# Loading a transformer block's small inputs from the ACT queue at the start, ahead of the first weight tiles

## The reference

```python
# every sub-layer: x <- LayerNorm(ALPHA * x + gate(c) * f(x * (1 + scale(c)) + shift(c)))
def even_mixer(h, positions, w_in, conv_w, a_log, dt_bias, gdn_norm_w, sinks, w_out):
    a_qkv, a_z, a_a, a_b, b_q, b_k, b_v = split_cols(h @ w_in, EVEN_WIDTHS)
    a_qkv = jax.nn.silu(causal_conv(a_qkv, conv_w))
    ...
    g = -jnp.exp(a_log) * jax.nn.softplus(a_a + dt_bias)
    beta = jax.nn.sigmoid(a_b)
    o_a = gated_delta_rule(a_q, a_k, a_v, g, beta)
    ...
    q = rotary(b_q, positions, SWA_ROT_DIM, ROPE_THETA)
    ...
    o_b = sink_window_attention(q, k, v, sinks)
    return jnp.concatenate([o_a, o_b], -1) @ w_out
```

## Time and profile before

| | |
|---|---|
| median of 3 runs | 1677.35 us (1676.88 to 1677.6) |
| profiled execution, its own time | 1677.35 us |
| its span | 1675.4 us |
| TensorE busy | 1604.0 us, 96% |
| VectorE busy | 1289.5 us, 77% |
| ScalarE busy | 1009.6 us, 60% |
| GpSimd busy | 104.6 us, 6% |
| bytes moved | 515.33 MB, mean 308 GB/s |

### The profile page before, as it was taken

The page is one execution under the profiler, slowest core; times in us unless marked ns, Lnnn a source line. Parts: engine busy times, 40 slices in busy tenths (PEclk is TensorE's granted clock), DMA queues, the critical chain, the costliest instruction groups (busy, mean ns, idle before and its releaser), DMA issues.

```text
span 1675.4 us, 20080 instructions
## 1 busy us (share of the span) xinstructions
PE 1604.0 (96%) x7810; PEld 1288.9 (77%) x7810; DVE 1289.5 (77%) x1176; ACT 1009.6 (60%) x868; POOL 104.6 (6%) x78
## 2 busy tenths in 40 slices
PE   4999999999999999699999999999999999999996
PEld 1876766888778887488888888888888888888875
DVE  1766466755566666889899898898988898988987
ACT  1442335444445554477777777777777777777765
POOL 0003120200001102100000000000000000000004
PEclk9999999999999999799999999999999999999998
DMA  9688696855535445399999999999999999999993
GB/s 347 230 298 310 246 326 214 286 178 201 201 134 179 157 164 181 133 377 399 369 389 381 377 389 369 387 387 369 387 387 369 387 383 374 388 382 364 386 382 134
DMA packets 234370, 515.33 MB, mean 308 GB/s; under 512 B 8936, under 2 KB 40960, under 8 KB 234176
## 3 DMA queue, kind: packets, MB, share of 16 engines
q1 hardware_dynamic: 228688, 493.77, 80.5%
q0 software_dynamic: 3008, 10.20, 1.8%
q10 hardware_dynamic: 2576, 10.02, 1.7%
HBM read 507.15 MB, written 13.11 MB: 311 GB/s over the span
## 4 chain that ended last, share of the span: by engine, by line
PE 90%; DVE 4%; DMA 3%; ACT 1%; issue 1%; POOL 0%; ACTq 0%; POOLq 0%; SPq 0%; DVEq 0%
PE bank L756 27%; PE bank L758 27%; PE bank L757 27%; DMA ring<-in_cond_w 2%; PE bank L735 2%; PE bank L927 2%; PE bank L1193 1%; DMA small<-in_ev_w_in 1%; PE bank L1105 1%; PE bank L1175 0%; PE bank L751 0%; DVE w_lo L1681 0%; ACT hT_hi L1308 0%; PE bank L1184 0%; PE bank L988 0%
## 5 line engine op out<-in xcount | busy, mean ns | idle before, releaser
L1681 DVE TENSOR_TENSOR w_lo<-ring,w_hi 128x2048 fp32r<-128x2048 f32 x336 | 765.0, 2291 | 105.7 <-ACT w_hi L1566 104.2
L1566 ACT ACTIVATE w_hi<-ring 128x2048 fp32r<-128x2048 f32 x334 | 640.5, 1918 | 197.7 <-PE bank L758 188.6
L756 PE MATMUL bank<-w_lo,heT_hi 128*128 128x512 f32 x896 | 353.8, 395 | 3.7 <-DVE w_lo L1681 2.2
L758 PE MATMUL bank<-w_hi,heT_hi 128*128 128x512 f32 x896 | 349.7, 390 | 0.0
L757 PE MATMUL bank<-w_hi,heT_lo 128*128 128x512 f32 x896 | 348.8, 389 | 0.0
L1670 DVE TENSOR_TENSOR w_part<-ring,w_part 128x1024 fp32r<-128x1024 f32 (+1 forms) x162 | 201.4, 1252 | 160.2 <-ACT w_part L1319 157.3
L1319 ACT ACTIVATE w_part<-ring 128x1024 fp32r<-128x1024 f32 (+1 forms) x162 | 169.0, 1049 | 230.3 <-PE bank L758 210.6
L756 PEld LDWEIGHTS bank<-w_lo,heT_hi 128*128 128x128 f32 x896 | 168.3, 188 | 38.9 <-issue 5.9
L758 PEld LDWEIGHTS bank<-w_hi,heT_hi 128*128 128x128 f32 x896 | 168.2, 188 | 35.9
L757 PEld LDWEIGHTS bank<-w_hi,heT_lo 128*128 128x128 f32 x896 | 168.4, 188 | 33.7
L756 PE MATMUL bank<-w_part,hT_hi 128*128 128x512 f32 (+1 forms) x448 | 179.4, 400 | 6.0 <-DVE hT_lo L1661 4.8
(11 more groups left out here) (345 smaller groups left out, 1529.2 us busy)
## 6 DMA issues: line engine op xcount, KB each, us to landing
ring<-in_moe_w_up SPq DMA_DIRECT2D x224, 1024.0 KB, 8.6
ring<-in_moe_w_down SPq DMA_DIRECT2D x112, 1024.0 KB, 7.8
ring<-in_cond_w SPq DMA_DIRECT2D x24, 2048.0 KB, 9.5
ring<-in_ffn_w_up SPq DMA_DIRECT2D x22, 1024.0 KB, 8.5
ring<-in_od_w_in SPq DMA_DIRECT2D x8, 2048.0 KB, 7.9
ring<-in_ev_w_in SPq DMA_DIRECT2D x5, 2048.0 KB, 10.8
ring<-in_ffn_w_down SPq DMA_DIRECT2D x5, 2048.0 KB, 7.6
ring<-in_od_w_in SPq DMA_DIRECT2D x8, 1024.0 KB, 7.7
```

The costliest lines, as they stand in the source:

```text
L756: mm(bank, lhs[0], rhs[1], start=start, stop=False)
L758: return mm(bank, lhs[0], rhs[0], start=False, stop=stop)
L1566: f(w_hi[:, n % 3], half_landed(act, it, u, half), ACT.Copy) \
L1681: tt(w_lo[:, buf], at, w_hi[:, buf].bitcast(F32), ALU.subtract).then_inc(S["w_lo"], 1)
```

## The change

ACT issues five transfers as its first instructions: positions, the rest of the constants, xs, the convolution weights and ab_w. SP no longer issues xs and the constants, and POOL no longer waits for the fourth conditioning tile. The transpose of the convolution weights moves ahead of the turning of hs, on TensorE and in the written-out order. On DVE, the angles, nw_lo and the copy of the convolution weights come before modulate. On ACT, nw_hi comes before `cond_kept` and the sines before hT_hi.

```diff
--- before.py
+++ after.py
@@ -154,7 +154,7 @@
 def pe_order():
 
     o = [("cT",), ("cond_rows", 0)]
-    o += [("cond", 0, u) for u in FIRST_COND] + [("hT", 0, i) for i in range(4)] + [("abT",), ("ab",), ("convT",)]
+    o += [("cond", 0, u) for u in FIRST_COND] + [("convT",)] + [("hT", 0, i) for i in range(4)] + [("abT",), ("ab",)]
     o += [("ev_in", u, i) for u in range(3) for i in range(4)]
     o += [("ev_in", u, t) for u in (5, 4) for t in range(NT)] + [("l2",)]
     o += [("ev_in", 3, t) for t in range(NT)] + [("l2_row", i) for i in range(4)]
@@ -651,10 +651,6 @@
                 if before[key]:
                     slot_read(sp, before[key])
                 load(s, source(key))
-                if key == ("cond", 0, FIRST_COND[-1]):
-                    sp.dma_start(xs[:], x[0].rearrange("(t p) d -> p t d", p=P)).then_inc(S["x_in"], 16)
-                if key == ("ev_in", 0):
-                    sp.dma_start(cst[:, 2 * P:], consts[:, 2 * P:N_FIRST]).then_inc(S["consts_in"], 16)
 
             def expert_unit(e, u, a):
 
@@ -820,12 +816,12 @@
             cond_rows(len(FIRST_COND))
             for u in FIRST_COND:
                 cond(0, u)
+            pe.wait_ge(S["convw_in"], 16)
+            bank, full = to_fill(pe, "convT")
+            nc.tensor.transpose(bank[:, 0:48], conv_rows, ident[0:48, 0:48]).then_inc(full, 1)
             turn(0, h_ready(0))
             pe.wait_ge(S["nw_lo"], 1)
             narrow("ab", ab_rows)
-            pe.wait_ge(S["convw_in"], 16)
-            bank, full = to_fill(pe, "convT")
-            nc.tensor.transpose(bank[:, 0:48], conv_rows, ident[0:48, 0:48]).then_inc(full, 1)
 
             for u in range(3):
                 for j in range(4):
@@ -1271,14 +1267,15 @@
         @block.scalar
         def _(act):
             f = nc.scalar.activation
+            act.dma_start(posi[:], positions[0].rearrange("(t p) -> p t", p=P),
+                          allow_slow_non_contiguous=True).then_inc(S["positions_in"], 16)
+            act.dma_start(cst[:, 2 * P:], consts[:, 2 * P:N_FIRST]).then_inc(S["consts_in"], 16)
+            act.dma_start(xs[:], x[0].rearrange("(t p) d -> p t d", p=P)).then_inc(S["x_in"], 16)
+            act.dma_start(conv_rows, ev_conv_w[0].rearrange("j (c p) -> (j c) p", p=P)).then_inc(S["convw_in"], 16)
+            act.dma_start(ab_w, ev_w_in[0, :, QKV + GH * GD:QKV + GH * GD + 2 * GH]
+                          .rearrange("(k p) n -> p k n", p=P)).then_inc(S["abw_in"], 16)
             act.wait_ge(S["c_in"], 16)
             f(c_row, c_row, ACT.Silu).then_inc(S["c_act"], 1)
-            weights(act, "cond", 0, FIRST_COND[-1])
-            act.dma_start(ab_w, ev_w_in[0, :, QKV + GH * GD:QKV + GH * GD + 2 * GH]
-                          .rearrange("(k p) n -> p k n", p=P)).then_inc(S["abw_in"], 16)
-            act.dma_start(conv_rows, ev_conv_w[0].rearrange("j (c p) -> (j c) p", p=P)).then_inc(S["convw_in"], 16)
-            act.dma_start(posi[:], positions[0].rearrange("(t p) -> p t", p=P),
-                          allow_slow_non_contiguous=True).then_inc(S["positions_in"], 16)
 
             def cond(l, u):
 
@@ -1324,6 +1321,8 @@
 
             heads = lambda b: b[:].rearrange("p (h j) -> p h j", h=GH)
 
+            act.wait_ge(S["abw_in"], 16)
+            f(nw_hi[:], ab_w, ACT.Copy).then_inc(S["nw_hi"], 1)
             def cond_kept(b):
 
                 bank, free = filled(act, "cond_rows", b)
@@ -1332,15 +1331,14 @@
             cond_kept(0)
             for u in FIRST_COND:
                 cond(0, u)
-            act.wait_ge(S["abw_in"], 16)
-            f(nw_hi[:], ab_w, ACT.Copy).then_inc(S["nw_hi"], 1)
+
+            for i in range(2):
+                act.wait_ge(S["angle_ready"], i + 1)
+                f(trig[:, i], ang[i], ACT.Sin).then_inc(S["trig_ready"], 1)
             turned(0)
             split_to(BUFS)
             copy(("abT",), ab_rows, lambda b: b[0:NE, 0:SEQ])
             copy(("ab",), ab, lambda b: b[:, 0:NT * NE].rearrange("p (t n) -> p t n", t=NT))
-            for i in range(2):
-                act.wait_ge(S["angle_ready"], i + 1)
-                f(trig[:, i], ang[i], ACT.Sin).then_inc(S["trig_ready"], 1)
             act.wait_ge(S["gates_in"], 32)
             act.wait_ge(S["gate_in"], 2)
             f(g_a, g_a, ACT.Exp, scale=-1.0).then_inc(S["gate_exp"], 1)
@@ -1780,14 +1778,14 @@
                 dve.wait_ge(S["nw_hi"], n)
                 tt(nw_lo[:], w, nw_hi[:].bitcast(F32), ALU.subtract).then_inc(S["nw_lo"], 1)
 
+            turns()
+            narrow_lo(ab_w, 1)
+            bank, free = filled(dve, "convT")
+            nc.vector.tensor_copy(conv_w, bank[:, 0:48]).then_inc(free, 1)
             dve.wait_ge(S["x_in"], 16)
             modulate(0, 0)
-            narrow_lo(ab_w, 1)
             turned(0)
             split_to(BUFS)
-            bank, free = filled(dve, "convT")
-            nc.vector.tensor_copy(conv_w, bank[:, 0:48]).then_inc(free, 1)
-            turns()
             taken(dve, "ab")
             dve.wait_ge(S["gates_in"], 32)
             as8 = lambda a: a.rearrange("p (t h) -> p t h", t=NT)
@@ -2276,7 +2274,6 @@
             tt = nc.gpsimd.tensor_tensor
             quad = lambda a, t: a[:, GH * t:GH * t + GH]
             G = Steps(pool, S["pool_step"])
-            weights(pool, "cond", 0, FIRST_COND[-1])
             pool.dma_start(alog, ev_a_log.broadcast_to([P, GH])).then_inc(S["gates_in"], 16)
             pool.dma_start(dtb, ev_dt_bias.broadcast_to([P, GH])).then_inc(S["gates_in"], 16)
             pool.dma_start(sinks, ev_sinks.broadcast_to([P, SH])).then_inc(S["sinks_in"], 16)
```

## The result

The changed kernel takes 1685.66 us (median of 5 runs beside 1676.88 for the kernel before, measured together); the ratio is 1.0054, with a 95% interval of 1.0043 to 1.0065: 8.8 us slower. The forecast was 1680.4 with a range up to 1683.5, so the time lies outside it, on the slower side. The profiled execution took 1683.41 us, with a span of 1681.5.

A forecast was written before the change was run, and what follows sets the result against it. Taken as bound by TensorE, 96% busy, so a delayed start reaches the end unshortened. +5.3 - 0.25 - 1.5 - 0.15 - 0.3 = +3.1 us on 1677.35 gave 1680.4 us, range 1676.5 to 1683.5.

The forecast's parts named there:

- Part 1, the push: Start: five transfers ahead of the conditioning weights make the fourth conditioning tile land 5.3 us later, bounds 3.6 and 6.2.
- The term for the bytes: Start: 1.90 MB moved ahead at 389 GB/s takes 4.9 us from the conditioning tiles.
- the idle room: Spare DMA bandwidth from 2 to 4 us, expected to absorb 0.6 us of the push, bounds 0 and 1.3.
- The term for small elements: Start: small elements cost 1.0 us beyond their bytes, bounds 0 and 1.3, from the 309 GB/s row.
- Parts 2, 3, 6 and 7: Silu hidden; ab_w early, so hT_lo follows modulate; convT transpose moved, 0.15 us gained; third weight part's wait gone, 0.3 gained.
- part 6: Before the first projection: the convT transpose leaves, 0.15 us of its 0.26 counted as gained.
- Part 4: Before modulate: DVE's conv_w copy, waiting for a transpose behind all conditioning products, starts modulate 1.44 us later.
- Parts 3 and 4: Before the gate product: ab_w's wait removed, conv_w copy's wait added; hT_lo ends earlier, net gain 0.25 us.
- Part 5, the clock: Gate product: TensorE's idle stretch shrinks from 3.7 to 2.0 us, so full clock; 1.5 us gained, bounds 0 and 1.5.
- The premise: Gate product: the length of the idle stretch before it sets the clock; 2.0 us taken as short enough for full clock.
- the small-transfer term: Start: small elements' cost beyond their bytes, 1.0 us, bounds 0 and 1.3.

## Why the prediction was wrong, step by step

*Part 1, the push, is the step that failed in size: 8.4 us where 5.3 was forecast and 6.2 was the bound.* That transfers issued ahead of the critical tile push it back by their bytes was right. The term for the bytes held: xs and the constants cost 3.6 us net of the idle room (4.6 - 0.6 = 4.0 by the prediction's terms). The term for small elements, 1.0 with a bound of 1.3, was mis-sized: the small transfers alone cost 3.8 us. It was read from the row at 309 GB/s, of a stretch in which the same transfers ran beside other things, and it was booked to element size and number. The runs show another cause: the 128-fold read of one row. The norm weight alone costs 2.45 us, the four 3.2, ab_w with its 1024 elements 0.43, and the same shape from different rows nothing that can be told from scatter. The row misled in two ways. It is a mean rate, and with the norm weight alone the mean rate accounts for 1.0 of the 2.45 us by which the tile was late. And late, beside the running stream, the same reads were cheaper: POOL's four held 8.6% of the engines' time from 26 to 36 us in the kernel before, 0.86 us of all engines, against the 2.7 us at the start of the changed kernel. Why they cost more at the start no run shows. POOL's four stood in the prediction with half a sentence, as bytes. With their wait put back the push is 4.8 us, inside the forecast's bounds of 3.6 and 6.2.

The large and the small alone add up to 3.58 + 3.79 = 7.4 us; together they cost 8.4. Each of the single runs had the idle room at the start to itself: over the first 4 us the large ones alone moved 0.35 MB more than the kernel before (158 GB/s against 70), the changed kernel only 0.12 MB more (101 GB/s). That would be 0.6 of the 1 us; it is argued, not shown.

*The Trainium skill's rule that weighed against the change* (the Trainium skill, "DMA: Bandwidth & Descriptors", Issuing engines are not separate DMA queues), that the transfers of all issuing engines run on the same 16 DMA engines, agrees with the traces: xs and the constants from ACT pushed the ring back by 3.6 us, and POOL's four transfers cost 2.3 us from ACT and 3.2 from POOL.

*Parts 2, 3, 6 and 7 held.* Silu was hidden: TensorE waited for the tile, 12.8 us of the 19.9 before the first group. ab_w landed at 19.95 (2.75 + 17.2), ahead of need by far. hT_lo followed modulate directly. The wait for the third part is gone. For part 6, the end of the stretch in the kernel before, and then in the changed one:

```profile
47.82 0.29 PE L815 MATMUL bank<-cst,arena 8*128 8x8 f32 x2 [0.46 <-ACT arena L1301]
...
48.23 0.38 PE L756 MATMUL bank<-hT_lo,w_part 128*128 128x256 f32 x1
```

```profile
56.30 0.29 PE L811 MATMUL bank<-cst,arena 8*128 8x8 f32 x2 [0.46 <-ACT arena L1298]
56.52 0.39 PE L752 MATMUL bank<-hT_lo,w_part 128*128 128x256 f32 x1
```

Between these two it took 0.41 us and then 0.22, so the transpose that left this place gave 0.19 us (0.15 forecast). From the start of the gate product to its read-back it took 5.05 us instead of 4.89, because more of it ran at half clock; so the whole stretch is only 0.03 us shorter.

*Part 4 held.* Modulate came 8.40 us after the fourth group (8.36 forecast), and with the copy behind it the gate product starts 1.36 us earlier (1.44 forecast). Parts 3 and 4 together gave 0.10 us of the 0.25 forecast.

*Part 5, the clock, failed too: 0.16 us lost instead of 1.5 gained.* The idle stretch before the gate product shrank to 1.7 us and the clock was at 0.50 all the same; it had fallen at 48 to 49 us, within the transposes (1.75 us instead of 1.26). The new wait of part 4 had also made the stretch before the first transposes 2.23 us long (1.08 before), which the prediction didn't count. The premise, that the length of the last stretch decides, is wrong: after 1.7 us of it the product ran at half clock here, after 3.22 us at the full clock in the run with 20 extra transposes. With waits between 1.7 and 2.7 us before the gate product, one trace had the full clock throughout (ab_w alone), the others lost it before or within the product. The product ran at the full clock in both kernels with extra transposes, one trace of each. The Trainium skill ("TensorE: Matmul & The Clock Gate", What's actually happening) has it that the throttled state is the default and activity releases it; granted clock 1.00 behind the extra transposes is in line with that, but the trace with ab_w alone had it without them. What decides it stays open.

In sum for the first projection, read from the traces: +8.42 push, -0.10 for parts 3 and 4, -0.19 for part 6, +0.16 for the clock, together 8.29: 56.52 instead of 48.23 us. At 133 us the lag is 7.8, so some 0.5 us came off in between; the wait for the third part, which is gone, is 0.3 of it. The medians are 8.8 apart. Where the last 1 us of that lies, and what makes the steps between 133 and 1639 us, stays open; the clock falls at other points in the two traces (from 260 to 290 us it was 0.94 before and 1.00 after).

*The range* failed because both ends of the small-transfer term were too low: 0, and a value from one row, whose stretch held the repeated reads late and behind the critical tile. The upper end with this term at 3.8 us instead of 1.3 would have held the time.

## What to carry to other kernels

A transfer issued early is free only if the DMA engines have room before the first thing that somebody waits for; here they had 2 us. Replicating a small vector over partitions by transfer cost many times its bytes here (2.45 us for 64 KB), whichever engine issued, so it belongs behind the critical loads. A mean rate over a stretch is not the delay of one tile in it; to price the delay, look at when the tile lands. Before moving a load, see whether the instruction that waits for it can be moved instead: here two small instructions placed behind the work that doesn't need them let the gate product start 1.1 us earlier with nothing pushed back, though only 0.3 us of it was left at the first projection.

## What the runs showed of the hardware

128 reads of 512 bytes from one HBM row, beside a full weight stream, made a tile of that stream land 2.45 us later (348 GB/s from 4 to 12 us; 18.0 us of time summed over the 16 DMA engines, longest packet 2.46 us). The same bytes from 128 rows made it 0.1 us later, which is within scatter (388 GB/s; 5.6 us, longest packet 0.72 us). 1024 elements of 32 bytes from different rows cost 0.43 us. Two large queues beside each other ran at 393 GB/s, as fast as one. TensorE's clock for the same instructions differed between traces of kernels with the same start: the fourth group of products took between 1.92 and 3.64 us. The gate product ran at half clock after TensorE had been idle for 1.68 us in one kernel, and at the full clock after 3.22 us in another.
